# Expert down weights loaded with four rows in one stretch per partition, gate and up lanes reading every fourth column

## The chip, the cores and the metric

The kernel runs on one core of a Trainium2 chip. The metric is the device time of one execution in microseconds (us). A core has a matrix engine (PE, with its weight loads listed apart as PEld), a vector engine (DVE), a scalar engine (ACT), GpSimd (POOL), a sync engine (SP) that issues transfers here, and 16 DMA engines that carry the transfers.

## The reference

The program is two transformer blocks in float32. The first has two layers, each ending in a layer of 32 experts, of which every token uses two. In layer 0 the experts see 512 tokens, in layer 1 256 tokens. What one expert computes, and the widths:

```python
D_MODEL = 1024; EXPERT_HIDDEN = 512; N_EXPERTS = 32; TOP_K_INNER = 2
# grouped_experts: the tokens are sorted by expert, xb are the rows of one expert e
def run(args):
    xb, e = args
    return (jax.nn.silu(xb @ w_gate[e]) * (xb @ w_up[e])) @ w_down[e]
```

`w_gate` and `w_up` are 1024 x 512, `w_down` is 512 x 1024, so each of the three matrices of an expert has 2 MB. All weights of all experts are read once per layer: 192 matrices in all. The rest of the program (convolution mixer, attention, a state-space branch, a sparse attention, a feed-forward block) is not touched by the change.

## The kernel before, in words

**The ring.** All large weights pass through `ring`, six slots of 2 MB in SBUF (`RING = 6`, `SLOT = 4096` floats per partition). `chunk(n, k, cols)` is slot `n % 6` seen as `k` rows of `cols` columns per partition. Three consecutive slots hold gate, up and down of one expert, so two experts fit. SP issues one transfer per matrix (`experts`, L2141 to L2168): the first two experts ahead of the layer, the others in a loop over pairs of experts. Before it issues a transfer it waits until PE has finished the last product that reads the slot (`finished`, a semaphore per kind of matrix).

**Where the rows of a matrix go.** With `"e (p k) n -> e p k n"` (gate, up) partition `p` takes the eight consecutive rows 8p to 8p+7 of the matrix, which is one stretch of 16 KB in memory. With `"e (k p) n -> e p k n"` (down, L2146) partition `p` takes the rows p, 128+p, 256+p and 384+p, which are four stretches of 4 KB.

**The expert loop.** The tokens of an expert are worked on in chunks of at most 32 (`CAP`). PE runs, per chunk (L534 to L571): the gate product into `bank[0]`, the first half of `combine` for the chunk before, the up product into `bank[1]`, `dispatch` (L496, gathers tokens for a later chunk), a transpose of the hidden values (L566), the second half of `combine` (L517) and the down product into `bank[2]`.

**Four lanes.** The tokens are the stationary operand and have only 32 columns, so `four_lanes` (L541 to L548) splits the array into four column strips ("lanes"). Lane m multiplies the same 32 tokens with another quarter of the matrix's columns and writes to partitions 32m to 32m+31 of the bank. The weights are the moving operand. In the gate product lane m reads columns 128m to 128m+127 of each row:

```python
last = pe.matmul(b[32 * m:32 * m + 32, 0:width], lhs[:, k, :],
                 rhs[:, k, m * width:(m + 1) * width],
                 start=(k == 0), stop=(k == nk - 1), tile_position=(0, 32 * m))
```

A float32 product shows up in the trace as two records of PE, so the gate product (8 rows x 4 lanes) has 64 records, the up product 64, and the down product (4 rows x 4 lanes) 32 of double width. All of them carry line L545.

**The hidden values.** ACT and DVE make `hid` from the two banks (`silu(gate) * up`); row 32m+s of it holds token s and the 128 hidden values of lane m. PE transposes it (L566), ACT copies it to `hid_t`; block m of `hid_t` then has on partition x the hidden value of lane m, column x. The down product takes block k together with row k of the down matrix's slot, so partition x of both must mean the same hidden index: 128k + x before.

Elsewhere, ACT's copy of the tokens in `moe` (L1739, L1740) writes its results to SBUF with a distance of 128 floats between neighbouring elements; the first copies of the program (into `x_t`) write neighbouring elements side by side. Both read PSUM and move 128 x 512 floats.

Of the kernel before, what the change touches and what calls it, by code (L numbers as in the profile page):

```python
# [17 lines left out]
P = 128  # L18
D = 1024
KD = D // P  # L20
# [6 lines left out]
HID = 512  # L27
# [88 lines left out]
def two_blocks(nc, w, out):  # L116
# [7 lines left out]
    with ExitStack() as ctx:  # L124
# [35 lines left out]
        bank = [banks[:, 512 * i:512 * i + 512] for i in range(8)]  # L160
        V_BANKS, A_BANKS = bank[:4], bank[4:]

        def v3(t, off, a, b):
            return t[:, off:off + a * b].rearrange("p (a b) -> p a b", a=a)
# [32 lines left out]
        def conv_chunk(j):  # L197
            return EARLY + 3 * j - (j == 5) * 2
# [38 lines left out]
        y_sb, xe = b12[:, 7680:7936], v3(b12, 7936, KD, CAP)  # L237
        spread = v3(b3, 0, 4, 512)
        disp_at = 2048
        silu_g, hid, hid_t = [b3[:, 3072 + P * i:3200 + P * i] for i in range(3)]  # L240
# [63 lines left out]
        def _(pe):  # L304
# [111 lines left out]
            def moe(layer, tiles, pieces=((), (), ())):  # L416
# [67 lines left out]
                if pieces[2]:  # L484
# [3 lines left out]
                s = {k: sem(f"{k}{layer}") for k in ("disp_ready", "xq_full", "xq_taken", "xe_taken", "hq_ready",  # L488
                                                      "gate_full", "up_full", "hid_ready", "hidt_full", "hidt_taken", "y_full",
                                                      "y_taken", "comb_ready", "part_full", "part_added")}  # L490
# [36 lines left out]
                with pe.Fori(0, NE // 2) as pair:  # L527
                    for j in range(2):
                        e = pair * 2 + j
                        cs = [n0 + 3 * j + i for i in range(3)]  # L530
                        wg, wu, wd = chunk(cs[0], KD, HID), chunk(cs[1], KD, HID), chunk(cs[2], 4, D)

                        lower, upper = (bound[0], bound[1]) if j == 0 else (bound[1], bound[2])
                        with pe.Fori(lower, upper):  # L534
                            n = pe.snap(chunk_no)
                            pe.reg_add(chunk_no, chunk_no, 1)

                            def expert_loaded(i):
                                pe.wait_ge(slot_loaded[cs[i] % RING], pair * 16 + 16 * (cs[i] // RING + 1))

                            def four_lanes(b, lhs, rhs, nk, width):  # L541

                                for k in range(nk):
                                    for m in range(4):
                                        last = pe.matmul(b[32 * m:32 * m + 32, 0:width], lhs[:, k, :],  # L545
                                                         rhs[:, k, m * width:(m + 1) * width],
                                                         start=(k == 0), stop=(k == nk - 1), tile_position=(0, 32 * m))
                                return last  # L548

                            expert_loaded(0)  # L550
                            pe.wait_ge(s["xe_taken"], n + 1)
                            if j == 0:
                                pe.reg_load(bound[2], cum[0:1, bass.ds(e + 2, 1)])
                            else:
                                pe.reg_load(bound[0], cum[0:1, bass.ds(e + 1, 1)])
                                pe.reg_load(bound[1], cum[0:1, bass.ds(e + 2, 1)])
                            four_lanes(bank[0], xe, wg, KD, P).then_inc(s["gate_full"], 1)
                            combine(n, 0)
                            expert_loaded(1)
                            four_lanes(bank[1], xe, wu, KD, P).then_inc(s["up_full"], 1)  # L560
                            pe.wait_ge(s["disp_ready"], n * 2 + 16)
                            pe.wait_ge(s["xq_taken"], n + 4)
                            pe.wait_ge(s["hq_ready"], n + 1)
                            dispatch(bank[3], lambda t, kk: v3(h_q, 0, 4, 256)[:, t, kk * P:(kk + 1) * P], ((n + 4) % 8 // 4) * (tiles * P))
                            pe.wait_ge(s["hid_ready"], n + 1)
                            pe.transpose(bank[0][:, 0:P], hid, ident).then_inc(s["hidt_full"], 1)  # L566
                            combine(n, 1)
                            expert_loaded(2)
                            pe.wait_ge(s["hidt_taken"], n + 1)
                            pe.wait_ge(s["y_taken"], n + 1)  # L570
                            four_lanes(bank[2], hid_t.rearrange("p (k s) -> p k s", k=4), wd, 4, 256).then_inc(s["y_full"], 1)  # L571
                combine(total, 0)
                combine(total, 1)

# [40 lines left out]
            p = EARLY  # L615
            for j, which in enumerate("vaava"):
                n = conv_chunk(j)
# [13 lines left out]
            n = conv_chunk(5)  # L631
# [40 lines left out]
            n = start["middle"] + 6  # L672
# [81 lines left out]
            n = start["after"] + 2  # L754
# [164 lines left out]
            for t in range(2):  # L919
                for half in range(2):  # L920
                    pe.wait_ge(sem("final_ready"), 4 * half + 4)
                    b = bank[1 + 2 * t + half]
# [1189 lines left out]
        def _(sp):  # L2112
# [28 lines left out]
            def experts(layer):  # L2141
# [1 line left out]
                n0 = start[f"moe{layer}"]  # L2143
                ws = [w["expert_w_gate"][layer].rearrange("e (p k) n -> e p k n", p=P),
                      w["expert_w_up"][layer].rearrange("e (p k) n -> e p k n", p=P),
                      w["expert_w_down"][layer].rearrange("e (k p) n -> e p k n", p=P)]  # L2146
                for j in range(6):
                    v, a = read_by[n0 + j - RING]
                    sp.wait_ge(v_full, v)
# [135 lines left out]
```

## Time and profile before

| | us |
|---|---|
| three timed runs | 2091.21, 2092.39, 2087.99 |
| their median | 2091.21 |
| the profiled execution, its own time | 2092.63 |
| its span, first to last instruction | 2090.8 |
| experts of layer 0, PE's L545 | 335.4 to 817 |
| experts of layer 1, PE's L545 | 1099.4 to 1557 |

The profile is one execution. Its page gives each engine's busy time, the span in 40 slices of 52 us with the busy share in tenths, and groups of instructions by line and shape. The granted clock of PE was 0.938 of full speed on average. Other views of the same trace list waits, the chain of work that ended last, instructions in order of time, and busy times of chosen stretches. Where PE is "busy", its records overlap: the pace of a group is read from how many records start in how much time.

### The profile page before, as it was taken

Reading aid. Unit: us, or ns where it says so; the run is one execution under the profiler, and the core shown is the slowest. Engines: PE = TensorE matmul, PEld = TensorE weight load, DVE = VectorE, ACT = ScalarE, POOL = GpSimd, SP = SyncE. Lnnn points to the kernel's source line nnn. Section 1 sums busy time; section 2 is a strip of 40 time slices with the busy share of each in tenths; the row PEclk is TensorE's granted clock in tenths of the full one; section 3 lists DMA queues with packets and bytes.
Section 4 is the critical chain, followed back from the end, with each engine's and each line's share of the span. In section 5 each row is a group of like instructions: output and inputs, shape, how many; then the busy total and the mean of one; then the engine's idle time right before and its main releaser. Section 6 shows DMA issues by size and latency. Waiting matters only on the chain.

```text
span 2090.8 us, 56358 instructions
## 1 busy us (share of the span) xinstructions
PE 1841.8 (88%) x23140; PEld 1315.6 (63%) x23141; DVE 899.5 (43%) x2115; ACT 592.0 (28%) x1230; POOL 549.6 (26%) x407
## 2 busy tenths in 40 slices
PE   5999978999999998898989986766667989899998
PEld 3454456666666665655676754545445777778886
DVE  2098145555555555445343432222234995210001
ACT  1001153333333333314343432222223324120001
POOL 0000004666666663001004432222238000100000
PEclk8999988999999999999989998898877999999999
DMA  9664164989999999932079999999992355533320
GB/s 374 235 242 161 40 236 185 381 339 422 420 422 418 421 419 404 347 107 71 21 269 412 400 419 424 420 424 420 425 409 91 121 217 187 201 121 121 132 90 21
DMA packets 133060, 574.35 MB, mean 275 GB/s; under 512 B 4720, under 2 KB 9840, under 8 KB 116464
## 3 DMA queue, kind: packets, MB, share of 16 engines
q1 hardware_dynamic: 132688, 570.72, 69.0%
q10 hardware_dynamic: 288, 2.43, 0.3%
q8 instruction: 62, 1.02, 0.2%
q14 instruction: 22, 0.18, 0.0%
HBM read 572.08 MB, written 1.05 MB: 274 GB/s over the span
## 4 chain that ended last, share of the span: by engine, by line
PE 68%; DMA 16%; DVE 7%; ACT 4%; issue 3%; SPq 1%; DVEq 0%; ACTq 0%
PE bank L339 25%; PE bank L545 18%; DMA ring<-in_expert_w_gate 12%; PE bank L517 6%; PE bank L496 6%; PE bank L909 4%; ACT b L1670 2%; DVE b L949 2%; PE bank L593 2%; DMA ring<-in_expert_w_down 2%; PE bank L827 1%; PE bank L410 1%; DMA ring<-in_ada_w 1%; DMA ring<-in_expert_w_up 1%; DVE h_t L949 1%
## 5 line engine op out<-in xcount | busy, mean ns | idle before, releaser
L545 PE MATMUL bank<-ring,b 128*32 128x128 f32 (+1 forms) x13600 | 528.2, 309 | 118.7 <-issue 48.4
L545 PEld LDWEIGHTS bank<-ring,b 128*32 128x32 f32 x13600 | 401.5, 115 | 301.2 <-issue 210.8
L949 DVE TENSOR_TENSOR h_t<-h_t,bank 128x512 f32<-128x512 f32 (+1 forms) x696 | 350.7, 566 | 500.0 <-PE bank L517 500.0
L1670 ACT ACTIVATE b<-bank 128x128 f32<-128x128 f32 (+3 forms) x554 | 193.9, 377 | 1157.5 <-PE bank L496 403.6
L339 PE MATMUL bank<-h_t,ring 128*128 128x256 f32 (+1 forms) x1664 | 453.6, 435 | 6.9 <-DVE h_t L1453 3.6
L339 PEld LDWEIGHTS bank<-h_t,ring 128*128 128x128 f32 x1664 | 321.4, 194 | 132.4 <-issue 94.2
L2068 POOL TENSOR_SCALAR b<-b 128x1024 f32<-128x1024 f32 (+1 forms) x85 | 195.1, 2295 | 63.5 <-POOL b L2076 37.2
L2076 POOL TENSOR_TENSOR b<-b 128x512 f32<-128x512 f32 (+1 forms) x85 | 89.1, 1048 | 429.4 <-PE bank L517 429.4
L517 PE MATMUL bank<-b 32*128 32x512 f32 (+1 forms) x1392 | 172.7, 567 | 5.4 <-DVE h_t L949 4.7
L2071 POOL TENSOR_TENSOR b<-b,b 128x1024 f32<-128x1024 f32 (+1 forms) x85 | 161.2, 1896 | 7.1
L1670 ACT ACT_TABLE_LOAD x109 | 139.8, 1283 | 10.9 <-DMA par<-in_params 9.0
L496 PE MATMUL bank<-b 128*128 x1064 | 142.3, 284 | 0.0
L496 PEld LDWEIGHTS bank<-b 128*128 128x128 f32 x1064 | 126.1, 193 | 17.4 <-issue 17.4
L949 DVE TENSOR_TENSOR b<-b,bank 128x128 f32<-128x128 f32 (+3 forms) x124 | 41.9, 342 | 196.6 <-PE bank L339 151.6
L1670 ACT ACTIVATE b<-b 128x256 f32 (+5 forms) x186 | 107.7, 622 | 28.2 <-DVE b L949 14.9
L2054 POOL MEMSET h_t<- 128x512 f32 (+1 forms) x16 | 5.9, 420 | 396.6 <-ACTq L1742 396.6
L517 PEld LDWEIGHTS bank<-b 32*128 32x128 f32 x1392 | 57.2, 193 | 41.3 <-issue 34.8
L339 PE MATMUL bank<-b,ring 128*128 128x256 f32 (+1 forms) x256 | 71.3, 441 | 6.6 <-issue 3.7
L1226 DVE SCALAR_TENSOR_TENSOR b<-b,par,b 128x512 f32<-128x512 f32 x116 | 76.9, 749 | 0.0
L909 PE MATMUL bank<-b,ring 128*128 128x256 f32 x352 | 76.2, 379 | 0.5 <-DVE b L949 0.5
L909 PEld LDWEIGHTS bank<-b,ring 128*128 128x128 f32 x352 | 66.8, 190 | 10.0 <-DVE b L949 0.9
L339 PE MATMUL bank<-ring,h_t 128*128 128x512 f32 (+2 forms) x192 | 68.3, 515 | 3.2 <-ACT h_t L1670 1.7
(270 smaller groups left out, 1459.7 us busy)
## 6 DMA issues: line engine op xcount, KB each, us to landing
ring<-in_expert_w_gate SPq DMA_DIRECT2D x64, 2048.0 KB, 13.9
ring<-in_expert_w_up SPq DMA_DIRECT2D x64, 2048.0 KB, 15.9
ring<-in_expert_w_down SPq DMA_DIRECT2D x64, 2048.0 KB, 16.2
ring<-in_ada_w SPq DMA_DIRECT2D x24, 2048.0 KB, 19.7
ring<-in_w_mod SPq DMA_DIRECT2D x12, 2048.0 KB, 7.9
ring<-in_w_in SPq DMA_DIRECT2D x6, 2048.0 KB, 12.4
ring<-in_conv_w_in SPq DMA_DIRECT2D x5, 2048.0 KB, 9.1
ring<-in_w_ffn_gate SPq DMA_DIRECT2D x5, 2048.0 KB, 8.0
```

The source lines that it names most:

```text
L339: last = pe.matmul(o, lhs(k), rhs(k), start=(k == 0), stop=(k == nk - 1))
L496: last = pe.matmul(b[:, kk * P:(kk + 1) * P], part(t, kk), b3[:, bass.ds(disp_at + t * P + buf, P)], start=(t == 0), stop=(t == tiles - 1))
L517: pe.matmul(bank[4 + j][:, 0:ntok], y_sb[32 * j:32 * j + 32, half * P:(half + 1) * P], comb_t[32 * j:32 * j + 32, 0:ntok], start=True, sto ...
L545: last = pe.matmul(b[32 * m:32 * m + 32, 0:width], lhs[:, k, :], rhs[:, k, m * width:(m + 1) * width], start=(k == 0), stop=(k == nk - 1), ...
L593: last = pe.matmul(b[32 * j:32 * j + 32, 0:P], c[:, k, :], wt[:, k, j * P:(j + 1) * P], start=(k == 0), stop=(k == KD - 1), tile_position= ...
L909: last = pe.matmul(bank[m][:, 0:SEQ], wt[:, kk, m * P:(m + 1) * P], f_hid[:, k, :], start=(k == 0), stop=(k == KF - 1))
L949: return dv.tensor_tensor(o, a, b, op)
L1226: step(dv.scalar_tensor_tensor(o, src, wt, o, ALU.mult, ALU.add))
L1670: return ac.activation(o, i, f, **kw)
L2068: po.tensor_scalar(weighed[:, :, 0:ntok], spread[:, 0:2, 0:ntok], slot_id, None, ALU.is_equal) \
L2071: po.tensor_tensor(weighed[:, :, 0:ntok], weighed[:, :, 0:ntok], spread[:, 2:4, 0:ntok], ALU.mult) \
L2076: po.tensor_tensor(comb_t[:, 0:ntok], weighed[:, 0, 0:ntok], weighed[:, 1, 0:ntok], ALU.add) \
```

## The change

The down matrix is loaded with `(p k)` like the other two, so partition p gets its rows 4p to 4p+3 in one stretch of 16 KB. Then block k of the hidden values must hold hidden index 4x + k on partition x. To get that, lane m of the gate and of the up product no longer reads 128 neighbouring columns but the columns m, m+4, m+8 and so on: neighbouring elements of the moving operand lie 16 bytes apart. `four_lanes` gets a function that gives the columns of a lane; the down product still reads 256 neighbouring columns per lane.

```diff
-                            def four_lanes(b, lhs, rhs, nk, width):
+                            def four_lanes(b, lhs, rhs, nk, width, lane_cols):
 
                                 for k in range(nk):
                                     for m in range(4):
                                         last = pe.matmul(b[32 * m:32 * m + 32, 0:width], lhs[:, k, :],
-                                                         rhs[:, k, m * width:(m + 1) * width],
+                                                         rhs[:, k, lane_cols(m)],
                                                          start=(k == 0), stop=(k == nk - 1), tile_position=(0, 32 * m))
                                 return last
 
+                            every_fourth = lambda m: slice(m, HID, 4)
...
-                            four_lanes(bank[0], xe, wg, KD, P).then_inc(s["gate_full"], 1)
+                            four_lanes(bank[0], xe, wg, KD, P, every_fourth).then_inc(s["gate_full"], 1)
...
-                            four_lanes(bank[1], xe, wu, KD, P).then_inc(s["up_full"], 1)
+                            four_lanes(bank[1], xe, wu, KD, P, every_fourth).then_inc(s["up_full"], 1)
...
-                            four_lanes(bank[2], hid_t.rearrange("p (k s) -> p k s", k=4), wd, 4, 256).then_inc(s["y_full"], 1)
+                            four_lanes(bank[2], hid_t.rearrange("p (k s) -> p k s", k=4), wd, 4, 256,
+                                       lambda m: slice(m * 256, (m + 1) * 256)).then_inc(s["y_full"], 1)
...
-                      w["expert_w_down"][layer].rearrange("e (k p) n -> e p k n", p=P)]
+                      w["expert_w_down"][layer].rearrange("e (p k) n -> e p k n", p=P)]
```

The list of instructions of SP, in the loop over pairs of experts, before (the shape behind a transfer is partitions x stretches x elements):

```order
L2165 DMA ring<-in_expert_w_gate 128x4096
L2165 DMA ring<-in_expert_w_up 128x4096
L2165 DMA ring<-in_expert_w_down 128x4x1024
L2157 REGISTER_ALU
```

and with the change, where two added lines shift the line numbers by two:

```order
L2167 DMA ring<-in_expert_w_gate 128x4096
L2167 DMA ring<-in_expert_w_up 128x4096
L2167 DMA ring<-in_expert_w_down 128x4096
L2159 REGISTER_ALU
```

The down transfer has one stretch per partition instead of four; nothing else moves. PE, DVE, ACT and POOL have the same instructions in the same order as before.

## Rows read from the trace of the kernel before

**Rows 1.** The page: span, PE busy, 40 slices of PE and DMA.
```profile
span 2090.8 us, 56358 instructions
PE 1841.8 (88%) x23140; PEld 1315.6 (63%) x23141; DVE 899.5 (43%) x2115; ACT 592.0 (28%) x1230; POOL 549.6 (26%) x407
...
PE   5999978999999998898989986766667989899998
...
DMA  9664164989999999932079999999992355533320
```

**Rows 2.** Stretches of both expert stages: busy us, clock, DMA share, GB/s.
```profile
600.00:650.00 50.00, 49.73 (x968) 34.49 (x967) 28.61 (x56) 19.31 (x35) 33.68 (x21) 1.00 1.01 420
...
1150.00:1200.00 50.00, 49.52 (x1125) 37.90 (x1114) 22.17 (x67) 20.60 (x42) 22.62 (x24) 1.00 0.97 397
...
1300.00:1350.00 50.00, 34.63 (x612) 25.36 (x604) 13.21 (x40) 13.21 (x27) 15.01 (x16) 0.86 1.02 425
```

**Rows 3.** Waits from 360 to 800 us: the longest that PE's units have.
```profile
PEld bank L545 <- issue: 88.4, 132, 0.8
...
PEld bank L517 <- issue: 16.1, 88, 0.2
```

**Rows 4.** Waits from 1120 to 1520 us, PE's on transfers.
```profile
PE bank L545 <- DMA ring<-in_expert_w_gate: 35.3, 10, 3.6
...
PE bank L545 <- DMA ring<-in_expert_w_down: 19.2, 18, 1.3
```

**Rows 5.** Chain that ended last, layer 1: start, us, what.
```profile
1460.20 25.43 DMA ring<-in_expert_w_gate
...
1490.58 24.89 DMA ring<-in_expert_w_gate
```

**Rows 6.** Timeline of PE, layer 1: start, us, line, shape, records, idle before.
```profile
1471.34 3.50 PE L545 MATMUL bank<-ring,b 128*32 128x128 f32 x64 [3.53 <-DMA ring<-in_expert_w_gate]
...
1475.66 1.95 PE L545 MATMUL bank<-ring,b 128*32 128x128 f32 x64 [0.18 <-DMA ring<-in_expert_w_up]
...
1480.78 1.93 PE L545 MATMUL bank<-ring,b 128*32 128x256 f32 x32 [1.32 <-DMA ring<-in_expert_w_down]
```

**Rows 7.** SP's down transfers issued from 1170 to 1530 us.
```profile
L2165 SPq DMA_DIRECT2D ring<-in_expert_w_down x26: 383/383/384, 1170.4 to 1527.6; - x26
```

**Rows 8.** Timeline of PE and its weight loads, the last chunks of layer 0.
```profile
786.97 1.95 PE L545 MATMUL bank<-ring,b 128*32 128x128 f32 x64
...
796.88 1.95 PE L545 MATMUL bank<-ring,b 128*32 128x128 f32 x64
...
801.92 1.93 PE L545 MATMUL bank<-ring,b 128*32 128x256 f32 x32
...
806.11 1.95 PE L545 MATMUL bank<-ring,b 128*32 128x128 f32 x64 [2.25 <-issue]
...
809.93 1.95 PE L545 MATMUL bank<-ring,b 128*32 128x128 f32 x64 [0.80 <-DMA ring<-in_expert_w_up]
...
815.07 1.45 PEld L545 LDWEIGHTS bank<-ring,b 128*32 128x32 f32 x32 [0.85 <-DMA ring<-in_expert_w_down]
```

**Rows 9.** Gate and up records of PE by shape, 335 to 822 us.
```profile
L545 PE MATMUL bank<-ring,b 128*32 128x128 f32 x6144 | 187.6, 274 | 5.1 <-issue 2.2 <-DMA ring<-in_expert_w_up 0.8
```

**Rows 10.** The same records from 1099 to 1228 us.
```profile
L545 PE MATMUL bank<-ring,b 128*32 128x128 f32 x1920 | 60.1, 277 | 3.3 <-issue 3.0
```

**Rows 11.** Timeline of PE: 32 records of 512 columns without lanes.
```profile
90.61 13.90 PE L339 MATMUL bank<-h_t,ring 128*128 128x512 f32 x32
```

**Rows 12.** ACT's copies by shape: 288 to 297.5 us, then 10 to 22 us.
```profile
L1670 ACT ACTIVATE b<-bank 128x512 f32<-128x512 f32 x8 | 7.2, 1077 | 1.9 <-PE bank L410 1.9
...
L1670 ACT ACTIVATE x_t<-bank 128x512 f32<-128x512 f32 x4 | 2.4, 598 | 6.5 <-PE bank L410 6.5
```

## The prediction

> **What bounds the kernel now.** I read the page first: PE is busy for 88% of the span, but the DMA slices stand at 9 for both expert stages, and in the second of them PE drops to 6 and 7 [rows 1]. So the stages have to be read one by one, in stretches. In layer 0 (600 to 650 us) PE is busy for 49.73 of 50 us while the DMA engines are at 1.01 of their time: both are full. At the start of layer 1 (1150 to 1200 us) it is much the same, PE at 49.52. After that (1300 to 1350 us) PE has work for only 34.63 of 50 us and the DMA engines stay at 1.02 with 425 GB/s [rows 2].
>
> The waits say who holds whom. From 360 to 800 us PE waits for no transfer; its idle time is only "issue", in pieces of 0.8 us and less [rows 3]. PE's own pace sets layer 0. From 1120 to 1520 us the matmuls wait for gate and down matrices to land [rows 4], and the chain that ended last runs through the transfers themselves: a gate transfer ends at 1460.20 + 25.43 = 1485.63 us, the one two experts later at 1490.58 + 24.89 = 1515.47 us [rows 5]. That is 29.84 us for two experts, 14.92 us for one. The transfers set the pace of layer 1.
>
> **What the longer stretch is worth.** The landing of each matrix can be read from the matmuls that wait for it. Up starts at 1475.66 us and down at 1480.78 us, both straight out of a wait for their transfer [rows 6]: the down transfer took 5.12 us of the DMA engines' time. From there to the next gate (1485.63 us) it is 4.85 us. With 14.92 us per expert and 5.12 for down, gate and up take 4.90 each. All three have 2 MB; gate and up come in 128 stretches, down in 512. With the change the down transfer has the form of the other two, so I price it at 4.90 and the saving at 0.22 us per expert.
>
> [...]
>
> In layer 1, the down transfers that SP issues from 1170.4 us on are 26 [rows 7]. In that stretch DMA is the bound (its share is 0.97 before 1200 us and 1.02 after), so the saving reaches the end of the stage in full: 26 x 0.22 = 5.7 us. The down matrices of the first experts there land while PE is the bound, and count nothing.
>
> In layer 0 only the end can move. Up groups start at 786.97 and 796.88 us, a chunk every 9.91 us. The last chunk breaks that pace: its down product starts at 815.07 us, where 801.92 + 9.91 = 811.83 us was due, and each of its three groups came out of a wait [rows 8]. So 3.24 us are lost to late transfers, and that is the most that can come back. The least is what the last three experts' down transfers give, 3 x 0.22 = 0.7 us, if the queue ran empty before them, since a transfer can't start before its slot is free. I take 2.0, the middle. The forecast gain is 5.7 + 2.0 = 7.7 us.
>
> **What the strided reads cost.** Every gate and up product now reads its moving operand with neighbouring elements 16 bytes apart. No matmul of this trace does that, so the price is bounded from its nearest rows. At the full clock a group of 64 records takes 1.95 us [rows 6], 30.5 ns per record. Without lanes, 32 records of 512 columns take 13.90 us [rows 11], 0.848 ns per column, so a record of 128 columns streams for 109 ns, and four lanes side by side need one start every 27.1 ns. PE starts one every 30.5: a column may get 12% longer before the lanes feel it.
>
> The low end is a cost of 0; a gain is excluded, since the count of records, their columns and the pace of their starts stay. [...] ACT's copy with scattered writes takes 1077 ns, with adjacent ones 598 ns [rows 12], which is 0.94 ns more per element. Added to 0.848 that makes 1.78 ns per column, or 128 x 1.78 / 4 x 64 = 3.65 us per group. [...] The ACT rows are writes over 512 bytes, of another engine; the matmul's own rows say only that it takes a column every 0.85 ns. Between ends this far apart I take 0, since the step is the smallest that leaves a 16-byte piece and PE has 12% to spare, but it is close to even.
>
> [...] No row here shows a strided read of PE.
>
> **Other edits.** SP issues the same transfers in the same order; one issue of a down transfer takes 383 ns [rows 7] beside several us of waiting, so its length is of no account. The down product reads adjacent columns as before. `hid`, its transpose and the copies have the same shapes.
>
> **The sum.** The profiled execution took 2092.6 us (span 2090.8 and 1.8 around it), so the sum for it is 2092.6 - 7.7 = 2084.9. It was 1.4 us above the median 2091.2 of the timed runs; on their scale the forecast is 2083.5.
>
> **Rivals.**
> First, the saving is eaten. PE is the bound in layer 0, where 6144 records make 96 groups in 48 chunks [rows 9]. If a strided group costs 7.7 / 96 = 0.08 us more, 4% of it, all is given back: about 2091. The same time comes out if the down transfer stays at 5.12 because its stretches were not its cost. For it: nothing of the margin is needed. Against it: the 12% of slack.
>
> Second, slower: the gate and up lanes read at half speed. Place: L545 on PE, both layers. A group goes from 1.95 to 3.50 us and a chunk gets 3.1 us longer. Layer 0 is PE's all through: 48 x 3.1 = 149 us, less the 3.2 us of waiting at its end, 146. In layer 1 the records up to 1228 us are 1920, 15 chunks [rows 10], at 8.25 us each; with 11.35 they end at 1099 + 170 = 1269 us. From there the DMA engines still have 21 experts of 14.7 us, 309 us, which ends near 1578 instead of 1557: 21 us. In the sum 167 us: 2258. With the ACT row's price it is 3.4 us per chunk, 163 - 3 + 25 = 185 us: 2276. It decides from 4% more per group on and is in full force at 80%. For it: the ACT rows. Against it: those rows are writes, of another engine and 512 bytes apart instead of 16. A partial form (groups 5 to 60% longer) lies between, 2095 to 2190. Beyond it, if the four lanes also had to take turns at the memory, a group would take 64 x 128 x 1.78 ns = 14.6 us and the kernel over 3000 us; I give that and everything above 2280 little.
>
> Third, the change doesn't do what it says: SP's transfer would still be cut in pieces. The gate transfer has the same shape and shows 4.90, so I don't count it apart.
>
> **How the numbers follow.** Forecast (gain of 4.5 to 10 us) 0.48; eaten or no saving (within 4 us) 0.09; partial slowing 0.12; half speed 0.25; beyond 0.06. The forecast's own range is 2080 to 2088: 0.7 to 3.2 us in layer 0, 5 to 6 in layer 1, and the timed runs' spread of some 2 us to both sides. The range of 8 in 10 has to reach into the other sign: 2080 to 2270 holds the forecast, the small cases, the partial one and about two thirds of half speed. What a measurement of this kernel can tell from no change is about 0.2%, 4.2 us. Faster by more than that: 0.47. Within it: 0.10. Slower: 0.43.
>
> **What would show it.** In the new profile: up-to-down landing in layer 1 at 4.90 and the gate landings of two experts 29.4 us apart instead of 29.84; 64 records of L545 in 1.95 us at full clock; the last wait of layer 0 shorter than 3.24 us in all; layer 0 chunks still 9.9 us apart. The prediction is wrong if a full-clock gate group takes over 2.03 us, which shows first in the chunk pace of layer 0; then DMA's share there falls below 1 and PE's stays full. It is wrong in size if the down transfer doesn't get shorter.

## The result and the profile after

| | us |
|---|---|
| predicted | 2083.5 (2080 to 2270) |
| the changed kernel, median of 4 runs | 2306.57 (2306.35 to 2309.03) |
| the kernel before, median of 4 runs beside it | 2091.8 |
| ratio | 1.1032, 95% interval 1.1013 to 1.1051 |

The change costs 215 us, 10%. I had forecast a gain of 7.7 us and given "slower" a chance of 0.43; the time lies above my range. The profiled execution has a span of 2307.2 us where the one of before had 2090.8, a difference of 216.4 us, and the readings below are made against that.

The page of the changed kernel, with the same parts as [rows 1]; the DMA packet line is new here (packets, then how many are under which size):

```profile
span 2307.2 us, 56358 instructions
PE 2123.0 (92%) x23140; PEld 1400.2 (61%) x23141; DVE 910.1 (39%) x2115; ACT 592.3 (26%) x1230; POOL 551.7 (24%) x407
...
PE   5999879999999999989998999988887798989998
...
DMA  9653348557868778895305967999999228434320
...
DMA packets 108484, 574.35 MB, mean 249 GB/s; under 512 B 4720, under 2 KB 9840, under 8 KB 83696
```

The same line of the kernel before:

```profile
DMA packets 133060, 574.35 MB, mean 275 GB/s; under 512 B 4720, under 2 KB 9840, under 8 KB 116464
```

The 24576 packets fewer are 64 down transfers with 384 stretches less each: the transfers are no longer cut in four, and the third rival is out. PE has the same 23140 records and is busy 281 us longer. In the DMA slices the nines of layer 0 are gone (it reads 5 to 8 there), and only the later part of layer 1 still stands at 9. The stretches say it in numbers (columns as in [rows 2]):

```profile
600.00:650.00 50.00, 49.83 (x718) 29.97 (x715) 20.80 (x39) 13.54 (x24) 25.56 (x15) 1.00 0.69 274
...
1300.00:1350.00 50.00, 49.56 (x769) 31.08 (x765) 15.81 (x48) 14.57 (x30) 16.14 (x18) 1.00 0.89 368
...
1600.00:1650.00 50.00, 42.28 (x643) 26.69 (x639) 12.38 (x37) 10.58 (x22) 11.29 (x12) 0.91 1.00 428
```

In layer 0 PE is as full as before and gets 718 records done in 50 us instead of 968, while the DMA share fell from 1.01 to 0.69. PE became slower and the transfers idle beside it. At 1600 us the share is 1.00: there the transfers are the bound again. Which records are slower is told by the groups, first both shapes over the whole run, then gate and up of layer 0 alone (335 to 1005 us), against [rows 9]:

```profile
L545 PE MATMUL bank<-ring,b 128*32 128x128 f32 x10880 | 658.3, 408 | 46.9 <-issue 27.2 <-DMA ring<-in_expert_w_gate 17.3
...
L545 PE MATMUL bank<-ring,b 128*32 128x256 f32 x2720 | 164.4, 382 | 2.9
```

```profile
L545 PE MATMUL bank<-ring,b 128*32 128x128 f32 x6144 | 371.5, 408 | 2.1
```

The 6144 gate and up records of layer 0 were busy for 187.6 us and are now for 371.5, 184 us more. The down records, which read neighbouring columns, still take 164.4 us in all. The timeline of PE in layer 0 has the size of one group and the pace:

```profile
604.97 3.87 PE L545 MATMUL bank<-ring,b 128*32 128x128 f32 x64
608.77 2.05 PE L496 MATMUL bank<-b 128*128 x16
610.66 0.27 PE L567 MATMUL bank<-con,b 128*128 128x128 f32 x1
610.87 1.14 PE L517 MATMUL bank<-b 32*128 32x512 f32 x8
611.93 5.82 PE L545 MATMUL bank<-ring,b 128*32 128x256 f32 x96
617.68 1.14 PE L517 MATMUL bank<-b 32*128 32x512 f32 x8
618.75 3.87 PE L545 MATMUL bank<-ring,b 128*32 128x128 f32 x64
```

An up group takes 3.87 us where it took 1.95 ([rows 6, 8]), and the next one starts 618.75 - 604.97 = 13.78 us later, where a chunk took 9.91 to 10.0. (The row x96 is a down group and the next gate group, which the view puts together: 5.82 - 1.93 = 3.89.) Of the things between the groups, dispatch (L496), the transpose and combine (L517), none changed.

Where the 216.4 us lie can be read from the starts of L545's first and last record in each layer:

| profiled execution | before layer 0 | layer 0 | between | layer 1 | behind | span |
|---|---|---|---|---|---|---|
| before | 335.4 | 481.2 | 282.7 | 457.6 | 533.9 | 2090.8 |
| changed | 337.9 | 661.7 | 277.7 | 494.3 | 535.5 | 2307.2 |
| difference | +2.6 | +180.5 | -5.0 | +36.7 | +1.6 | +216.4 |

The parts outside the layers moved by -5.0 to +2.6 us; among the other kernels below they differ by 1.4 to 4.6 us too, so nothing is read from them. Chunk by chunk (start of the gate group in the changed kernel less that in the kernel before, same chunk, us; 48 chunks in layer 0, 37 in layer 1):

| chunk | 0 | 20 | 46 | 47 | 48 | 55 | 62 | 67 | 76 | 84 |
|---|---|---|---|---|---|---|---|---|---|---|
| late by | 2.56 | 79.25 | 178.58 | 180.18 | 178.06 | 200.13 | 227.00 | 217.15 | 215.16 | 213.44 |

In layer 0 every chunk adds 3.84 us, but for the last, which adds 1.60: the kernel before waited for transfers there [rows 8], the changed one doesn't. In layer 1 chunks 49 to 62 add 3.7 to 3.9 us each except two; from 63 on the kernel before waits for its transfers (12.5 to 15.4 us a chunk) and the changed one, whose transfers ran ahead meanwhile, catches up until 67. From there on both go at the pace of the transfers, and the changed kernel gains (217.15 - 213.44) / 17 = 0.22 us per chunk. That is the saving of the load, where and as large as it was predicted, under a loss nearly thirty times its sum.

### The profile page after: what moved, and what is told of

It is laid out like the page before. It is cut to its first block, busy times and chain, and to the rows that moved or that the text cites. A ratio compares the mean times of both kernels' runs of the same rounds, so it can differ in the third digit from the quotient of the medians.

```text
span 2307.2 us, 56358 instructions
## 1 busy us (share of the span) xinstructions
PE 2123.0 (92%) x23140; PEld 1400.2 (61%) x23141; DVE 910.1 (39%) x2115; ACT 592.3 (26%) x1230; POOL 551.7 (24%) x407
## 2 busy tenths in 40 slices
DMA packets 108484, 574.35 MB, mean 249 GB/s; under 512 B 4720, under 2 KB 9840, under 8 KB 83696
## 3 DMA queue, kind: packets, MB, share of 16 engines
HBM read 572.08 MB, written 1.05 MB: 248 GB/s over the span
## 4 chain that ended last, share of the span: by engine, by line
PE 76%; DMA 10%; DVE 6%; ACT 4%; issue 3%; SPq 1%; DVEq 0%; ACTq 0%
PE bank L545 29%; PE bank L339 23%; DMA ring<-in_expert_w_gate 9%; PE bank L517 6%; PE bank L496 6%; PE bank L911 3%; ACT b L1672 2%; DVE b L951 2%; PE bank L595 2%; PE bank L829 1%; PE bank L410 1%; DMA ring<-in_ada_w 1%; DVE h_t L951 1%; PE bank L644 1%; DVE b L1488 1%
## 5 line engine op out<-in xcount | busy, mean ns | idle before, releaser
L545 PE MATMUL bank<-ring,b 128*32 128x128 f32 (+1 forms) x13600 | 820.9, 403 | 49.8 <-issue 27.2
L545 PEld LDWEIGHTS bank<-ring,b 128*32 128x32 f32 x13600 | 493.7, 123 | 392.5 <-issue 182.5
L517 PE MATMUL bank<-b 32*128 32x512 f32 (+1 forms) x1392 | 167.7, 551 | 5.4 <-DVE h_t L951 4.7
L496 PEld LDWEIGHTS bank<-b 128*128 128x128 f32 x1064 | 125.1, 191 | 36.8 <-issue 36.8
L496 PE MATMUL bank<-b 128*128 x1064 | 141.3, 283 | 0.0
L517 PEld LDWEIGHTS bank<-b 32*128 32x128 f32 x1392 | 55.1, 185 | 58.5 <-issue 52.1
```

The source lines that it names most:

```text
L496: last = pe.matmul(b[:, kk * P:(kk + 1) * P], part(t, kk), b3[:, bass.ds(disp_at + t * P + buf, P)], start=(t == 0), stop=(t == tiles - 1))
L517: pe.matmul(bank[4 + j][:, 0:ntok], y_sb[32 * j:32 * j + 32, half * P:(half + 1) * P], comb_t[32 * j:32 * j + 32, 0:ntok], start=True, sto ...
```

## The experiments

Two questions were put. The first is which edit costs what: by my sum, the new load should be worth 7.7 us whatever the lanes read. The second is why a read at every fourth column is slow. **Theory A**: each stream of columns has a limit of its own, one read of a 16-byte piece per so much time, whatever runs beside it. **Theory B**: the four lanes hinder each other, because side by side they read the same pieces. Differences are taken between medians of runs made together; the kernel before ran beside every experiment.

### The new load alone

```diff
-    every_fourth = lambda m: slice(m, HID, 4)
+    adjacent = lambda m: slice(m * P, (m + 1) * P)
...
-    four_lanes(bank[0], xe, wg, KD, P, every_fourth)
+    four_lanes(bank[0], xe, wg, KD, P, adjacent)
...
-    four_lanes(bank[1], xe, wu, KD, P, every_fourth)
+    four_lanes(bank[1], xe, wu, KD, P, adjacent)
```

> The new down load alone: four rows of w_down in one stretch per partition, the gate and up lanes reading adjacent columns as in the kernel before. The hidden columns then meet other rows of w_down than they belong to; the amount of work is the same. If the loss of the changed kernel is all in the strided reads, warm gate and up groups are back at 1.95 us, the chunk pace of layer 0 at 9.91 us, and the down transfer lands 4.90 us after the up transfer: 2084 us (26 x 0.22 + 2.0 = 7.7 us under the kernel before, ratio 0.9963). If the longer stretch brings nothing that reaches the end (rival: saving eaten), 2091 us, ratio 1.000. If the load itself carried part of the loss, over 2100 us.

Measured: 2084.41 us (median of 6), before 2091.21, ratio 0.997 (0.9958 to 0.9982): 6.8 us faster. The times predicted for the whole change are those of this half of it. Its packets are those of the changed kernel, 108484, in a span of 2083.3 us. PE's timeline in layer 1 shows the up-to-down spacing of landings, both groups right out of a wait for their transfer as in [rows 6]:

```profile
1466.53 1.95 PE L545 MATMUL bank<-ring,b 128*32 128x128 f32 x64 [1.72 <-DMA ring<-in_expert_w_up]
...
1471.42 1.93 PE L545 MATMUL bank<-ring,b 128*32 128x256 f32 x32 [1.10 <-DMA ring<-in_expert_w_down]
```

1471.42 - 1466.53 = 4.89 us, where it was 5.12. Layer 1 took 451.8 us against 457.6, 5.8 us less (5.7 were forecast), and layer 0 479.8 against 481.2, 1.4 less (2.0). All of the loss is therefore elsewhere.

### The strided reads alone

```diff
-    w["expert_w_down"][layer].rearrange("e (p k) n -> e p k n", p=P)]
+    w["expert_w_down"][layer].rearrange("e (k p) n -> e p k n", p=P)]
```

> The strided reads alone: down loaded with single rows per stretch as in the kernel before, gate and up lanes reading every fourth column. The hidden columns meet other rows of w_down than they belong to; the amount of work is the same. If the strided reads are the whole loss and the load only a gain: groups of 64 at 3.87 us, layer 0 pace 13.78 us, and as layer 1 is late for its transfers again, up to 7.7 us above the changed kernel: 2308 to 2314 us. If reads and load work against each other somewhere (strided reads slow only beside 16 KB stretches), the time is nearer to the kernel before: under 2200 us.

Measured: 2312.43 us (median of 4), ratio 1.1064 (1.1048 to 1.108), +221.2 us. Added to the -6.8 of the load it gives +214.4, the loss of the whole change (+215) within what the medians scatter. The two edits are independent. In layer 1 the same table as above reads 215.68 at chunk 67 and 215.61 at chunk 84: without the long stretches nothing is gained there. The expectation's other case, slow reads only beside 16 KB stretches, is out.

### The forms of a matmul by themselves

A kernel that only multiplies matrices which lie loaded, one line for each form; the two lines that say what "side by side" and "512 apart" mean:

```python
v = lambda first, step, n: wt[:, first:first + (n - 1) * step + 1:step]
pe.matmul(bank[3][32 * m:32 * m + 32, 0:P], xs[:, 32 * k:32 * k + 32], v(512 * k + m, 4, P), ..., tile_position=(0, 32 * m))      # L51
pe.matmul(bank[4][32 * m:32 * m + 32, 0:P], xs[:, 32 * k:32 * k + 32], v(512 * (k + m), 4, P), ..., tile_position=(0, 32 * m))    # L56
```

> Only matmuls, no part of the reference is computed: groups of one form each from matrices that lie loaded, with no transfer running. Each lane form is 128 matmuls of 128 columns (four lanes of 32 output rows, two lanes, or one), each form without lanes 64 matmuls of 128 columns. Theory A, a limit of each stream: one read of a 16-byte piece gives at most two elements, or one stream at step 4 has a pace of its own whatever runs beside it. Then one lane alone at step 4 takes as long per matmul as step 1 or more, a plain matmul of 128x128 at step 4 takes about 1.9 ns a column where step 1 takes 0.85 (64 matmuls: 15 against 7 us), and the four lanes are as slow 512 floats apart as side by side. Theory B, the four lanes hinder each other because they read the same 16-byte pieces at the same time: side by side at step 4 the 128 matmuls take 7.7 us, 512 floats apart they are back at 3.9 us (or near it), and plain matmuls show no difference at step 4. Steps 2 and 3 and the runs of two tell what width counts: if a piece of 8 bytes or less is the unit, step 2 is as slow as step 4; if 16 bytes, step 2 lies at 3.9 us or between, step 3 between step 2 and step 4, and two of every four costs no more than step 2. If something else than width, steps 8 and 32 differ from step 4.

PE's timeline; from 58 to 515 us the granted clock is 1.00 and the DMA share 0.00. With lanes, in this order: step 1, 2, 3, 4 side by side, 4 with lanes 512 floats apart, 8, 32; then two of every four columns, two of every eight, four of every eight, two lanes at step 4, one lane at step 4, one lane at step 1:

```profile
58.17 7.19 PE L36 MATMUL bank<-wt,xs 128*32 128x128 f32 x256
65.18 7.63 PE L41 MATMUL bank<-wt,xs 128*32 128x128 f32 x256
72.56 11.45 PE L46 MATMUL bank<-wt,xs 128*32 128x128 f32 x256
83.76 15.03 PE L51 MATMUL bank<-wt,xs 128*32 128x128 f32 x256
98.57 15.03 PE L56 MATMUL bank<-wt,xs 128*32 128x128 f32 x256
113.33 15.28 PE L61 MATMUL bank<-wt,xs 128*32 128x128 f32 x256
128.28 22.56 PE L66 MATMUL bank<-wt,xs 128*32 128x128 f32 x256
150.55 7.67 PE L71 MATMUL bank<-wt,xs 128*32 128x128 f32 x256
157.99 7.68 PE L76 MATMUL bank<-wt,xs 128*32 128x128 f32 x256
165.42 7.24 PE L81 MATMUL bank<-wt,xs 128*32 128x128 f32 x256
172.40 29.22 PE L86 MATMUL bank<-wt,xs 128*32 128x128 f32 x256
201.42 58.20 PE L91 MATMUL bank<-wt,xs 128*32 128x128 f32 x256
259.45 28.13 PE L96 MATMUL bank<-wt,xs 128*32 128x128 f32 x256
```

Without lanes, at steps 1, 2, 3, 4 and 8:

```profile
287.50 14.56 PE L100 MATMUL bank<-wt,xs 128*128 128x128 f32 x128
301.90 14.67 PE L104 MATMUL bank<-wt,xs 128*128 128x128 f32 x128
316.41 22.34 PE L108 MATMUL bank<-wt,xs 128*128 128x128 f32 x128
338.58 29.18 PE L112 MATMUL bank<-wt,xs 128*128 128x128 f32 x128
367.59 30.04 PE L116 MATMUL bank<-wt,xs 128*128 128x128 f32 x128
```

Theory B falls on three rows. A single lane at step 4 takes 58.20 us where it takes 28.13 at step 1; a matmul without lanes takes 29.18 against 14.56; and lanes 512 floats apart are exactly as slow as lanes side by side (15.03). The slow-down is in the stream of one matmul, about twofold each time. The lanes still work side by side: 256 records take 58.2 us in one lane, 29.2 in two, 15.0 in four.

From start to start (what comes before the next form, so without the run-out of the last record) the plain forms take 14.40, 14.51, 22.17, 29.01 and 29.86 us per 128 records of 128 columns: 0.88, 0.89, 1.35, 1.77 and 1.82 ns per column of a record. One number gives them within 3%: 1.77 ns for each 16-byte piece that is read, and never less than 0.88 ns per column. Step 1 has four columns in a piece and takes 4 x 0.88 = 3.5 ns for them, so there the column is the bound; step 2 has two (0.89), step 3 moves 12 bytes, three quarters of a piece (0.75 x 1.77 = 1.33; measured 1.35), from step 4 on each column has its own piece. Two of every eight columns, side by side in one piece, have jumps of 28 bytes between the pairs and still cost no more than step 2 (7.43 us from start to start in four lanes, step 2 took 7.38), so it is not the length of the jump that counts.

In four lanes the same holds with slightly other numbers, but for step 32. Step 1 takes 7.01 us (0.86 ns per column) and step 4 takes 14.81, or 1.81 ns per piece, 2% more than in one lane; step 8 takes 14.95, step 32 takes 22.27. Half of 1.81 is 0.90 ns per column, and step 2 takes just that (7.38 us). So in lanes step 2 is already bound by the pieces, 5% above step 1.

### Where a piece begins, and other engines

Single operations again, each on its own line, 64 matmuls without lanes or 4 copies of 512 columns.

> Only single operations on loaded matrices, no part of the reference is computed. In the kernel of forms a plain 128x128 matmul group of 64 took 14.40 us at steps 1, 14.51 at 2, 22.17 at 3, 29.01 at 4, 29.86 at 8 (starts apart), and two of every four or eight columns were as fast as side by side. Theory A (aligned pieces of 16 bytes, one read each 1.78 ns): two of every four from columns 0, 1 and 2 take 14.5 us, from column 3, where each pair lies across a boundary, 29 us; two of every eight across a boundary 29 us; step 2 from an odd column 14.5; steps 5, 6, 12, 16 29 to 30 us. Theory B (a limit by the distance of neighbours: more than 8 bytes of jump is slow, wherever it starts): the pairs take the same from all four columns, and step 3 and 4 differ as seen. Step 32 was slower still in lanes (22.3 us against 14.9): if its own bank or row is the reason, step 16 lies between and step 48 with 32. A stationary operand at step 2 is then free as well, at step 3 and 4 as the moving one. [...]

PE's timeline, all of it at a granted clock of 1.00. Step 1 from column 0 (L37) and from column 1 (L41), step 2 from column 1 (L45), step 4 from column 3 (L49), then steps 5, 6, 12, 16, 32 and 48 (L53 to L73):

```profile
57.99 14.45 PE L37 MATMUL bank<-wt,xs 128*128 128x128 f32 x128
72.28 14.46 PE L41 MATMUL bank<-wt,xs 128*128 128x128 f32 x128
86.58 14.67 PE L45 MATMUL bank<-wt,xs 128*128 128x128 f32 x128
101.09 29.17 PE L49 MATMUL bank<-wt,xs 128*128 128x128 f32 x128
130.09 29.62 PE L53 MATMUL bank<-wt,xs 128*128 128x128 f32 x128
159.53 29.20 PE L57 MATMUL bank<-wt,xs 128*128 128x128 f32 x128
188.54 29.19 PE L61 MATMUL bank<-wt,xs 128*128 128x128 f32 x128
217.56 28.05 PE L65 MATMUL bank<-wt,xs 128*128 128x128 f32 x128
245.44 28.34 PE L69 MATMUL bank<-wt,xs 128*128 128x128 f32 x128
273.60 28.05 PE L73 MATMUL bank<-wt,xs 128*128 128x128 f32 x128
```

Two of every four columns from column 0 (L77), 1 (L81), 2 (L85) and 3 (L89), two of every eight from column 3, across a boundary (L93), every column twice (L97), then the stationary operand at steps 1, 2, 3, 4:

```profile
301.47 14.69 PE L77 MATMUL bank<-wt,xs 128*128 128x128 f32 x128
316.00 14.67 PE L81 MATMUL bank<-wt,xs 128*128 128x128 f32 x128
330.50 14.67 PE L85 MATMUL bank<-wt,xs 128*128 128x128 f32 x128
345.01 15.09 PE L89 MATMUL bank<-wt,xs 128*128 128x128 f32 x128
359.94 29.18 PE L93 MATMUL bank<-wt,xs 128*128 128x128 f32 x128
388.94 14.47 PE L97 MATMUL bank<-wt,xs 128*128 128x128 f32 x128
403.25 14.46 PE L101 MATMUL bank<-wt 128*128 128x128 f32 x128
417.54 15.24 PE L105 MATMUL bank<-wt 128*128 128x128 f32 x128
432.62 22.36 PE L109 MATMUL bank<-wt 128*128 128x128 f32 x128
454.81 30.03 PE L113 MATMUL bank<-wt 128*128 128x128 f32 x128
```

Two neighbours of every eight columns take 7.68 us in four lanes when they lie in one piece, half of what step 4 took there (15.03); across a boundary they take 29.18 us without lanes, as long as step 4 took there. The two rows differ in lanes too, but each is set against step 4 in its own form. So the pieces are aligned: their boundaries lie after every fourth column of `wt`, 16 bytes apart. Theory A's 1.78 ns a piece is what step 4 took with its run-out (29.18 us over 128 x 128 columns); from start to start it is 1.77. The pairs from columns 0, 1 and 2 took 14.69, 14.67 and 14.67 us and step 2 from an odd column 14.67, where 14.5 was expected; steps 5, 6, 12 and 16 took 29.62, 29.20, 29.19 and 28.05, where 29 to 30 was expected. Theory B's limit by distance is out: the pairs of every eight columns, with jumps of 28 bytes, took 7.68 us within a piece and as long as step 4 across a boundary. One of my figures was wrong: pairs from column 3 of four, which I expected at 29 us, take 15.09. They read pieces 0, 1, 1, 2, 2, 3, so each piece is still met twice in a row, one piece per two columns; I had counted a pair as two pieces and had not seen that the neighbouring pair shares one. The row fits the theory, the number that I worked out from it did not. The stationary operand has the same limit (14.46, 15.24, 22.36, 30.03). Steps 16, 32 and 48 take 28.05, 28.34 and 28.05 us, a little less than step 4 with 29.18 and step 8 with 30.04; in lanes only step 32 was run of the three, so what sets it apart there was not shown.

VectorE and ScalarE in the same trace, copying at steps 1, 2 and 4 (beside each other, while TensorE ran plain matmuls); step 8 took them as long as step 4 (2.24 and 4.18 us):

```profile
14.64 1.44 DVE L140 COPY tmp_v<-wt 128x512 f32<-128x512 f32 x4 [14.64 <-DMA xs<-in_x]
15.99 1.43 DVE L142 COPY tmp_v<-wt 128x512 f32<-128x512 f32 x4
17.34 2.22 DVE L144 COPY tmp_v<-wt 128x512 f32<-128x512 f32 x4
```

```profile
14.64 2.19 ACT L125 ACTIVATE tmp_a<-wt 128x512 f32<-128x512 f32 x4 [12.63 <-DMA xs<-in_x]
16.74 2.34 ACT L127 ACTIVATE tmp_a<-wt 128x512 f32<-128x512 f32 x4
18.98 4.27 ACT L129 ACTIVATE tmp_a<-wt 128x512 f32<-128x512 f32 x4
```

ScalarE doubles as well (1.03 to 2.03 ns a column, from start to start; the next form began at 23.14 us), VectorE rises from 0.66 to 1.05 (next form at 19.49). At step 2 VectorE takes as long as at step 1 (1.35 us from start to start) and ScalarE 7% longer (2.24 against 2.10). Whether the limit lies in the memory or in each engine's way to it, no run separates: ScalarE's doubling speaks for the memory, but it pays 2.03 ns per piece where TensorE pays 1.77.

### Every second column

Lane m reads every second column of one half, and w_down comes in two stretches of 8 KB, so that each column meets its row:

```diff
-    every_fourth = lambda m: slice(m, HID, 4)
+    every_second = lambda m: slice(m // 2 * 256 + m % 2, m // 2 * 256 + 256, 2)
...
-    w["expert_w_down"][layer].rearrange("e (p k) n -> e p k n", p=P)]
+    w["expert_w_down"][layer].rearrange("e (h p k) n -> e p h (k n)", h=2, p=P)]
```

> The reads of gate and up at step 2 in place of 4: w_down is loaded in two stretches of two rows (8 KB each) per partition, and lane m reads every second column of half m // 2. Nothing is left out. If a read of 16 bytes is the unit (step 2 took 7.38 us for 128 matmuls where step 1 took 7.01 and step 4 took 14.8, starts apart in the kernel of forms), the groups stay at 1.95 to 2.0 us, the layer 0 pace at 9.91 us, and what the load brings stays: with 8 KB stretches as good as 16 KB 2084 us, with half of the gain 2088 us. If a step of 2 costs in the kernel, where other engines use the memory too, in proportion to its width, the groups take 2.6 us or more, the layer 0 pace rises by 1.3 us a chunk, 48 x 1.3 = 62 us: 2150 us.

Measured: 2093.15 us (median of 11), before 2089.39, ratio 1.001 (1.0001 to 1.0019): no measurable change against the bound of 0.2%. The 220 us are gone with the step of 4, as theory A has it, but the time is 9 us above the 2084 that I expected for a full gain, and 5 above the 2088 for half of it. PE's timeline in layer 0:

```profile
601.12 2.04 PE L545 MATMUL bank<-ring,b 128*32 128x128 f32 x64
...
611.26 2.04 PE L545 MATMUL bank<-ring,b 128*32 128x128 f32 x64
```

A group takes 2.04 us, not 1.95, and a chunk 10.14 (9.97 on average with the new load and adjacent columns). Two groups x 0.09 x 48 chunks are 8.6 us; layer 0 took 487.4 us where the new load with adjacent columns took 479.8, 7.6 more. The forms had shown it (7.38 against 7.01 us for 256 records, 5%) and I had passed over it, though both numbers stand in the expectation. Layer 1 took 454.4 us, 3.2 less than before: the pace of two experts at its end is 15.26 + 14.31 = 29.57 us (chunks 83 and 84), with 4 KB stretches 15.39 + 14.44 = 29.83, with 16 KB 15.16 + 14.23 = 29.39. So 8 KB has 60% of what 16 KB brings.

### The change in layer 0 alone

```diff
+    every_fourth = lambda m: slice(m, HID, 4) if tiles == 4 else slice(m * P, (m + 1) * P)
...
+    ....rearrange("e (p k) n -> e p k n" if layer == 0 else "e (k p) n -> e p k n", p=P)]
```

> The whole change in layer 0 alone (load and lanes), layer 1 as in the kernel before. Nothing is left out. If each of layer 0's 48 chunks costs its two groups' 1.92 us more and nothing gives any of it back, 48 x 3.84 = 184 us: 2275 us, and the rest to the changed kernel (31 us) is layer 1. If the slower chunks of layer 0 let transfers catch up there that then no longer collide later, less: 2240 to 2260 us. If layer 1 had carried half of the loss (a strided read at the lower clock, late transfers behind it), 2200 us.

Measured: 2269.72 us (median of 4), ratio 1.0855 (1.0838 to 1.0872), +180.3 us. That is 5 us under the first case of the expectation and clear of the others. In its trace layer 0 took 662.0 us and layer 1 457.7, as before. The two layers' parts of the loss are 180 and, by difference to the whole change, 35 us; nothing of layer 0's comes back later.

### The transpose by VectorE in blocks

A way to have the new load without a strided matmul. The lanes read adjacent columns; VectorE transposes the hidden tile in 32x32 blocks and reads every fourth column while it does:

```diff
# PE
-    pe.wait_ge(s["hid_ready"], n + 1)
-    pe.transpose(bank[0][:, 0:P], hid, ident).then_inc(s["hidt_full"], 1)
# DVE
+    dv.wait_ge(s["hid_ready"], n + 1)
+    dv.transpose(hid_t, hid.rearrange("p (i k) -> p k i", k=4)).then_inc(s["hidt_taken"], 1)
# ACT
-    ac.wait_ge(s["hidt_full"], n + 1)
-    act(hid_t, bank[0][:, 0:P], ACT.Copy).then_inc(s["hidt_taken"], 1)
```

A block of 32x32 keeps lane m's values on partitions 32m to 32m+31: with column 4i + k read into block k, partition 32m + i holds hidden index 128m + 4i + k = 4(32m + i) + k, which is the row of w_down that the new load puts there.

> The new down load, gate and up lanes on adjacent columns, and the transpose of the hidden tile in another form, so that each column meets its own row of w_down: VectorE transposes it in blocks of 32x32 while it reads every fourth column, in place of the PE transpose and the ACT copy behind it. If the strided read costs VectorE no more than the ACT copy took and the saving of the load is real: PE loses its 0.1 to 0.2 us transpose in each of 96 chunks and the wait behind it stays what it was; 2075 to 2084 us, ratio 0.992 to 0.996. If the block transpose is long and later than PE wants it (it stands between the hidden tile and the down product, with two combine steps as cover), layer 0 loses what it exceeds the cover by: 1 us a chunk would be 48 us, 2130 us.

Measured: 2080.96 us (median of 6), before 2091.21, ratio 0.9954 (0.9941 to 0.9967). It is faster than the kernel before by 10.3 us. Against the new load alone, whose runs were made together with these, it is 3.5 us faster, and as the two intervals overlap that part is likely, not shown. The expectation counted 96 chunks; there are 85, as the count of the transposes says (96 are layer 0's groups). DVE's block transposes by shape:

```profile
L1155 DVE STREAM_TRANSPOSE b<-b 128x128 f32<-128x128 f32 x85 | 34.7, 409 | 2.9
```

They take 409 ns each, and nothing on PE waits for them: in layer 0 a chunk takes 9.81 us, 0.10 less than before, as PE's transpose is gone. By chunk 46 that is 4.7 us, of which the last chunk of the layer gives back 0.8 in waiting for transfers.

## Why the prediction was wrong

**The bound of each layer, right.** Layer 0 at PE's pace and layer 1 at that of the transfers: that is why 3.84 us per chunk reach the end in full in layer 0, and only partly in layer 1.

**The saving per down transfer, right.** 0.22 us was read from landings at 5.12 and 4.90; the load alone shows 4.89, layer 1 took 5.8 us less (forecast 26 x 0.22 = 5.7), and in the changed kernel itself the offset falls by 0.22 per chunk. The end of layer 0 gave 1.4 in place of 2.0 us. The sum of 7.7 us was measured as 6.8 (interval 3.8 to 8.8). Per expert layer 1 takes 29.83 / 2 us with 4 KB stretches in down, 29.57 / 2 with 8 KB, 29.39 / 2 with 16 KB.

**The cost of the strided reads, wrong.** This was the failing step, and it has two parts.

The first is "PE starts one every 30.5: a column may get 12% longer before the lanes feel it". The 12% were not there. I divided the 1.95 us of a group by its 64 records, and in a duration the last record's run-out is contained. The forms show it: 256 records take 7.19 us and 64 take 1.95, so 192 more cost 5.24, 27.3 ns each, and the 1.95 are 64 x 27.3 = 1.75 plus 0.20 of run-out. The 27.3 are what the lanes' own columns need (27.1, by my own division from [rows 11]): the lanes were already back to back, and any lengthening of a column was to be paid in full. Step 2 shows how finely: 5% more per column cost 7.6 us. The row that could have told it was at hand, the mean of one record in [rows 9], 274 ns: a record that takes 109 ns to stream has, by the profile's record ends, some 165 ns of run-out behind it, and a group has that once.

The second is the choice between a cost of 0 and a group of 3.5 to 3.65 us. The measured value is 3.87, near the high end. The ACT row that carried the high end [rows 12] is a write over a distance of 512 bytes, and with it I had got 1.78 ns per column; PE's own strided read takes 1.77. That I set it aside as being of another engine and kind was the error of judgement: it was the only row on the question, and there was none for a free step of 4. My other reason for 0, that the step is the smallest that leaves a 16-byte piece, had no row either, and it speaks for the high end: in the forms without lanes a column takes 1.70 to 1.82 ns from that step on (1.77 at step 4), where step 1 takes 0.88. That the two figures meet within 0.01 ns is luck all the same: I added what scattered writes cost ACT to PE's pace, and no run shows one cause behind both. The group then is 64 x 128 / 4 x 1.77 = 3.63 us plus the same 0.2 of run-out, 3.83. My 3.65 lacked the run-out, for the same reason as above.

1.77 ns per piece and never less than 0.88 per column give every row of the two kernels of forms within 5%, with lanes taken as side by side; only four lanes at step 32 fall out (22.3 us from start to start where 14.5 would be due).

**The second rival, right in kind, too low in size.** It had place, direction and point of decision. Its 3.1 us a chunk were 3.84: it left the run-out aside, and took for its price a group of adjacent columns at the low clock level (3.50 us [rows 6], granted clock 0.53). No run shows a strided group at 3.50 us; at step 4 it took 3.84 to 3.90 in those read here. The layer 0 term of 146 us was 180.5, that is 48 x 3.84 = 184.3 less the waits at the layer's end. The layer 1 term of 21 us was 36.7: PE is the bound for 4 chunks more than before, until chunk 67, and of the 49 us which the slow chunks of layer 1 add by chunk 62 only 9.9 come back there, besides the 3.7 of the shorter transfers. With 3.84 in its sum, the rival would have come out at 2304 us (184 - 3 in layer 0; 15 chunks of 8.25 + 3.84 end at 1280, with 309 us of transfers at 1589 instead of 1557, 32).

**The clock.** The rival took its price from a group at the low clock level. That left open whether the two would multiply, a strided read at the low level costing twice again. They don't. In the changed kernel a gate group behind an idle stretch of 3.01 us takes 3.90 us, the up group after it 3.84:

```profile
1671.61 3.90 PE L545 MATMUL bank<-ring,b 128*32 128x128 f32 x64 [3.01 <-issue]
...
1676.08 3.84 PE L545 MATMUL bank<-ring,b 128*32 128x128 f32 x64
```

The granted clock in those stretches (PE busy, clock, DMA share, GB/s behind the length):

```profile
1671.60:1675.50 3.90, 3.90 (x68) 0.66 0.99 420
1676.10:1679.80 3.70, 3.70 (x68) 1.00 1.00 425
```

With a clock of 0.50 in the first 2 us of the group (0.66 on average) it takes 3.90, at 1.00 throughout 3.84. Another, at 1701.01 us with the clock at 0.57 on average, took 3.88. In the kernel before, the gate group behind 3.53 us of idling took 3.50 us and the up group after it 1.95 [rows 6]; the clock in the gate group:

```profile
1471.40:1474.80 3.40, 3.40 (x68) 0.53 0.97 408
```

The pace of the strided read does not follow PE's clock between these levels, so at step 4 nothing is added where a group with adjacent columns took 1.55 us more.

**Chances.** 0.48 for the forecast against 0.31 for half speed and beyond was the weighing of a low end that no row supported against a high end for which the ACT row spoke; the group at the low clock [rows 6] only said what a doubling would come to. The range ended at 2270 because it was cut in the middle of that case, between its prices of 2258 and 2276. But the measured 2306.6 us lie above both, where I had left 0.06: the kind that came true had a chance of 0.25, its size hardly any.

## What to carry to other kernels

Before an operand of a matmul is read with a step, count the 16-byte pieces. From start to start, float32 at step 2 cost up to 5.5% here (without lanes 14.51 us against 14.40 at step 1, in four lanes 7.38 against 7.01, the stationary operand 15.08 against 14.29), at step 3 half more (22.17 against 14.40), from step 4 to 48 about double (27.9 to 29.9 without lanes), for the moving and the stationary operand alike (29.9 at step 4), and lanes hide nothing of it (14.81 against 7.01). If rows have to be permuted to make a transfer's stretches longer, do it where there is slack, on the small tile between the two products and not on the large operand: here VectorE's block transpose does it in 0.41 us a chunk, and the kernel comes out 0.46% faster instead of 10% slower. To find how much slack a pipelined group has, compare two lengths of the same group; a duration divided by its count contains the last one's run-out (0.20 of 1.95 us here) and shows slack that isn't there.

## What the runs showed of the hardware

- At the full clock TensorE reads its moving operand from SBUF at 0.88 ns per float32 column of a record or at 1.77 ns per aligned 16-byte piece, whichever is longer (29.01 us for 128 records of 128 columns at step 4, 14.40 at step 1); in four lanes at 0.86 and 1.81 (7.01 and 14.81 us for 256 records). The stationary operand has the same limit (14.46 us at step 1, 30.03 at step 4). Two of every four columns, where each piece is met by two columns in a row, cost what step 2 costs: 14.67 us within the pieces, 15.09 with the pairs across the boundary.
- The pace at step 4 doesn't follow the granted clock: 3.88 us for a group at 0.57, 3.90 at 0.66, 3.84 at 1.00. With adjacent columns a group took 3.50 us at 0.53 and 1.95 at 1.00.
- ScalarE has a like cliff at step 4 (2.10 to 4.16 us for four copies of 512 columns), VectorE a lower one (1.35 to 2.15); both copied at the same time.
- Four lanes at step 32 take 22.3 us from start to start where they take 14.8 at step 4, though without lanes step 32 is no slower (28.2 us against 29.0). So lanes can get in each other's way, at that distance and hardly at 4 (14.81 us where a quarter of one lane's 58.03 is 14.51); why stays open.
- The transfer of 2 MB in 16 KB, 8 KB and 4 KB stretches per partition goes at 4.89, 4.98 and 5.12 us, the middle one estimated from the pace of two experts: (29.57 - 29.39) / 2 = 0.09 more than 4.89.
